# Second block's FFN norm and the hybrid's successor get a head that runs ahead of the norm; the wait for masks stands later

## The reference, cut to what matters

```python
def rms_norm(x, g):
    y = x * lax.rsqrt(jnp.mean(x * x, axis=-1, keepdims=True) + EPS)
    return y * g
# first block, each sublayer: x + (half of) (1 + gate) * f(h), with
#   h = rms_norm(x, g) * (1 + scale) + shift
# f in turn: swiglu, hybrid (LRU and SSD), swiglu; swiglu, mLSTM, swiglu
def swiglu(h, w_gate, w_up, w_down):
    return (jax.nn.silu(h @ w_gate) * (h @ w_up)) @ w_down
# second block, behind its branches:
#   x = x + gate1 * rms_norm(mix, norm_mix_post)
#   h = rms_norm(x, norm_ffn_pre) * (1 + scale2) + shift2
#   x = x + gate2 * rms_norm(relu(h @ w_ff1)**2 @ w_ff2, norm_ffn_post)
```

## Time and profile before

| | us |
|---|---|
| median of 3 runs | 3580.46 |
| lowest and highest | 3576.4, 3591.96 |
| the profiled execution | 3580.06 |
| its span | 3578.2 |
| TensorE busy in it | 3448.2 |
| VectorE busy | 2018.7 |
| ScalarE busy | 1212.7 |

### The profile page before, as it was taken

The page is one execution under the profiler, slowest core; times in us unless marked ns, Lnnn a source line. Parts: engine busy times, 40 slices in busy tenths (PEclk is TensorE's granted clock), DMA queues, the critical chain, the costliest instruction groups (busy, mean ns, idle before and its releaser), DMA issues. The chain is left out here.

```text
span 3578.2 us, 56582 instructions
## 1 busy us (share of the span) xinstructions
PE 3448.2 (96%) x22456; PEld 2780.9 (78%) x22456; DVE 2018.7 (56%) x2820; ACT 1212.7 (34%) x1783; POOL 360.7 (10%) x264
## 2 busy tenths in 40 slices
PE   7999999999999999999999999999988999999998
PEld 5888777878888788876678888877757787878886
DVE  6666666846665666575443433365666773464343
ACT  3222346432222322243343322233434543233231
POOL 1000003410000000000101000130103330010000
PEclk9999999999999999999999999999979999989999
DMA  6554321125553455421032222222210002223232
GB/s 246 197 193 169 125 76 71 55 93 188 188 207 139 179 191 203 156 86 54 1 112 88 96 97 106 84 88 83 63 33 6 8 6 73 95 65 100 89 99 71
DMA packets 103765, 382.75 MB, mean 107 GB/s; under 512 B 11424, under 2 KB 15136, under 8 KB 103200
## 3 DMA queue, kind: packets, MB, share of 16 engines
q1 hardware_dynamic: 103584, 380.15, 30.7%
HBM read 378.01 MB, written 2.10 MB: 106 GB/s over the span
## 5 line engine op out<-in xcount | busy, mean ns | idle before, releaser
L457 PE MATMUL bank<-h_hi,w_hi 128*128 128x512 f32 x2576 | 1015.5, 394 | 29.2 <-DVE w_lo L252 26.5
L459 PE MATMUL bank<-h_hi,w_lo 128*128 128x512 f32 x2576 | 1005.6, 390 | 0.0
L458 PE MATMUL bank<-h_lo,w_hi 128*128 128x512 f32 x2576 | 1005.3, 390 | 0.0
L252 DVE TENSOR_TENSOR w_lo<-w_raw,w_hi 128x1024 fp32r<-128x1024 f32 (+2 forms) x480 | 634.3, 1321 | 397.7 <-ACT w_hi L246 386.5
L246 ACT ACTIVATE w_hi<-w_raw 128x1024 fp32r<-128x1024 f32 (+2 forms) x475 | 521.1, 1097 | 299.8 <-PE bank L459 260.4
L457 PEld LDWEIGHTS bank<-h_hi,w_hi 128*128 128x128 f32 x2576 | 485.3, 188 | 146.5 <-DVE w_lo L252 30.0
L459 PEld LDWEIGHTS bank<-h_hi,w_lo 128*128 128x128 f32 x2576 | 485.0, 188 | 102.4
L458 PEld LDWEIGHTS bank<-h_lo,w_hi 128*128 128x128 f32 x2576 | 485.5, 188 | 100.7 <-issue 1.9
L457 PE MATMUL bank<-f_gu_hi,w_hi 128*128 128x512 f32 x704 | 278.5, 396 | 0.0
L458 PE MATMUL bank<-f_gu_lo,w_hi 128*128 128x512 f32 x704 | 278.2, 395 | 0.0
L459 PE MATMUL bank<-f_gu_hi,w_lo 128*128 128x512 f32 x704 | 278.2, 395 | 0.0
(11 more groups left out here) (645 smaller groups left out, 4759.4 us busy)
## 6 DMA issues: line engine op xcount, KB each, us to landing
ada_tiles<-in_ada SPq DMA_DIRECT2D x180, 512.0 KB, 4.3
w_raw<-in_gu SPq DMA_DIRECT2D x176, 512.0 KB, 4.4
w_raw<-in_dn SPq DMA_DIRECT2D x64, 704.0 KB, 5.0
w_raw<-in_w_ff SPq DMA_DIRECT2D x64, 512.0 KB, 3.5
w_raw<-in_w_hyb SPq DMA_DIRECT2D x36, 512.0 KB, 3.4
w_raw<-in_w_rkv SPq DMA_DIRECT2D x24, 512.0 KB, 3.5
w_raw<-in_w_attn SPq DMA_DIRECT2D x20, 512.0 KB, 3.5
w_raw<-in_w_hout SPq DMA_DIRECT2D x16, 512.0 KB, 3.4
```

The source lines that it names most:

```text
L252: K.nc.vector.tensor_tensor(K.w_lo[:, half, 0:kb * P], K.w_raw[:, slot, 0:kb * P], K.w_hi[:, half, 0:kb * P].bitcast(F32), ALU.subtract).t ...
L457: nc.tensor.matmul(K.ps[bank][:], wh, hi, start=start, stop=False)
L458: nc.tensor.matmul(K.ps[bank][:], wh, lo, start=False, stop=False)
L459: last_mm = nc.tensor.matmul(K.ps[bank][:], wl, hi, start=False, stop=stop)
```

## The change

Four things. The swiglu behind the hybrid gets an early head: the last gemm of the hybrid makes the halves of x times gain ahead, in two regions that the hybrid has left. The second block's FFN gets one too, of a new class: its gain stands in `K.coef`, its squares are added between the products of its early tile (four sums for each chunk), its row comes behind the tile, and `norm` makes the halves ahead, chunk by chunk. In `gemm`, every early head now has the split of tile 3 in turn t = 0, ahead of tile 0's evacuation. And the wait for the RWKV masks is only in front of TensorE's first use of them.

```diff
                     if head and isinstance(i, int) and t < 3:
-                        if t < 2 and not (early and t == 0):
+                        if early and t == 0:
+                            split_lo(K, dve, kb, 3 % RING, 1, g0 + 3)
+                        elif t < 2 and not early:
                             split_lo(K, dve, kb, (t + 2) % RING, t % SPLIT, g0 + t + 2)
...
-                    hi, lo, bank, start, stop = mm(c, 0)
+                    _, _, bank, start, stop = mm(c, 0)
+                    hi, lo = head.ahead_hi[:, c, :], head.ahead_lo[:, c, :]
...
+class SecondModulated(Modulated):
+    def between(self, pe, n):
+        K, c, part = self.K, n // 3, n % 3
+        if part == 0:
+            pe.wait_ge(K.sq_done.sem, K.sq_done(c + 1 - DC))
+        for t in ((0, 1), (2,), (3,))[part]:
+            last = K.nc.tensor.matmul(K.ps[self.SUM][:, t:t + 1], self.squares.sq[0][:, c % 2, t * P:(t + 1) * P], K.ones[:, 0:1],
+                                      start=c == 0 and t == 0, stop=c == DC - 1, skip_group_check=True)
+        if part == 2:
+            last.then_inc(K.sq_added.sem if c < DC - 1 else K.rms_sum.sem, 1)
+        if DC <= n < 2 * DC:
+            self.shift_part(pe, n - DC)
+
+    def behind(self, pe):
+        self.row_of_roots(pe)
...
-            if squares:
-                squares.add_by_pe(pe).then_inc(K.rms_sum.sem, 1)
...
-                    nc.scalar.activation(squares.sq[0][:, c % 2:c % 2 + 1, :], K.x[:, c:c + 1, :], ACT.Square).then_inc(K.sq_done.sem, 1)
+                    nc.scalar.activation(follow.squares.sq[0][:, c % 2:c % 2 + 1, :], K.x[:, c:c + 1, :], ACT.Square).then_inc(K.sq_done.sem, 1)
+                    follow.ahead_act(act, c)
...
                 v.tensor_tensor(K.x[:, c, :], K.x[:, c, :], t[:, c, :], ALU.add).then_inc(K.x_written.sem, 1)
+                if follow and c:
+                    follow.ahead_dve(dve, c - 1)
...
@@ hybrid, last gemm
             squares.by_act(act, K.x[:, o:o + 1, :], o, o % 2)
+            follow.ahead_act(act, o)
...
             v.scalar_tensor_tensor(x, K.ps[HOUT_BANK[o]][:], K.coef[:, o:o + 1], x, ALU.mult, ALU.add).then_inc(free.sem, 1)
+            follow.ahead_dve(dve, o)
...
@@ second block
-    norm(K, "n2p", mix, col(K, "mix_post", 0, 8), gate=gt1, squares=Squares(K, "x2", K.h_at + 4 * S * 4))
-    head = Modulated(K, col(K, "ffn_pre", 0, 8), sc2, sh2)
+    head = SecondModulated(K, col(K, "ffn_pre", 0, 8), sc2, sh2, Squares(K, "x2", A))
+    norm(K, "n2p", mix, col(K, "mix_post", 0, 8), gate=gt1, follow=head)
...
@@ rwkv
-            dve.wait_ge(loaded, 16)
-            pool.wait_ge(loaded, 16)
-            pe.wait_ge(loaded, 16)
...
             def key_squares(i, x):
+                if i == 0:
+                    pe.wait_ge(loaded, 16)
```

More of the change, by code:

```diff
@@ L620, in add @@
             K.nc.gpsimd.tensor_tensor(self.acc[n][:], self.acc[n][:], self.sq[n][:, slot, :], ALU.add).then_inc(K.sq_added.sem, 1)
[L622 to L632, removed]
     def advance_pe(self):
@@ L850, in advance, with __init__, gain_ahead @@
             c.base += DC
+class SecondModulated(Modulated):
+    GAIN_STEPS = 0
+    def __init__(self, K, gain, scale, shift, squares):
+        super().__init__(K, gain, scale, shift, early=True)
+        self.gain_at, self.squares = K.coef, squares
+    def gain_ahead(self, dve):
+        K = self.K
+        K.nc.vector.scalar_tensor_tensor(K.coef[:], self.scale, 1.0, self.gain, ALU.add, ALU.mult).then_inc(K.coef_done.sem, 1)
+        dve.wait_ge(K.coef_done.sem, K.coef_done(1))
+    def between(self, pe, n):
[11 more added lines that the diff above has]
+        self.row_of_roots(pe)
 class FirstModulated(Modulated):
@@ L1128, in pool, with norm @@
             K.nc.gpsimd.tensor_scalar(K.x[:, c, :], K.x[:, c, :], self.final[:, c:c + 1], None, ALU.mult)
-def norm(K, name, src, gain, gate, squares=None, store=None):
+def norm(K, name, src, gain, gate, follow=None, store=None):
     nc = K.nc
@@ L1146, in _ @@
             rms.rms_act(act)
-            if squares:
+            if follow:
+                act.wait_ge(K.coef_done.sem, K.coef_done(1))
                 for c in range(DC):
@@ L1164, in _ @@
             v.tensor_tensor(K.gain[:], gain, gate, ALU.mult).then_inc(K.x_written.sem, 1)
+            if follow:
+                follow.gain_ahead(dve)
             rms.rms_dve(dve)
@@ L1171, in _ @@
                 v.tensor_tensor(K.x[:, c, :], K.x[:, c, :], t[:, c, :], ALU.add).then_inc(K.x_written.sem, 1)
+                if follow and c:
+                    follow.ahead_dve(dve, c - 1)
+            if follow:
+                follow.ahead_dve(dve, DC - 1)
     rms.rms_advance()
@@ L1174, in norm @@
     K.scaled.base += DC
-    if squares:
-        squares.advance_pe()
+    if follow:
+        follow.squares.advance_pe()
+        follow.ahead_advance()
+        K.coef_done.base += 1
 def swiglu(K, name, w_gu, w_down, nxt, head, gate, ada=None, double=False, follow=None):
@@ L1384, with hybrid @@
         ("lo_l", "rows", DC), ("n_sum", "e", 1), ("n_root", "bc", 1), ("n_rs", "fin", 1), ("n_row", "hi", 1), ("scaled", "zeroed", DC), ("hi_s", "trig", DC)]
-def hybrid(K, nxt, head, gate):
+def hybrid(K, nxt, head, gate, follow):
     nc, d = K.nc, K.dram
@@ L1788, in hybrid @@
     squares = Squares(K, "hyb", A + 2 * DC * CH)
+    follow.ahead_hi = K.at("hyb_ahead_hi", [P, DC, S], F32R, A + GATE * CH)
+    follow.ahead_lo = K.at("hyb_ahead_lo", [P, DC, S], F32R, A + Z * CH)
     def out_mm(k, j):
@@ L3735, in build @@
                 follow = final_head(K)
-            elif step != "hyb":
+            else:
                 follow = Modulated(K, *terms(K, *places[plan[n + 1]]), early=True)
@@ L3740, in build @@
                 with stage(K):
-                    hybrid(K, nxt, head, gate)
+                    hybrid(K, nxt, head, gate, follow)
             elif step == "ml":
```

17 lines of the change are left out of this document (9 added, 8 removed).

## The result

| | before | after |
|---|---|---|
| median us (9 runs each) | 3582.31 | 3603.7 |
| lowest and highest | 3576.4, 3593.84 | 3599.68, 3616.41 |
| span of the profiled execution | 3578.2 | 3597.9 |
| granted clock over the span | 0.983 | 0.982 |

The ratio is 1.0057, 95% interval 1.0044 to 1.0070: 20.4 us slower (15.8 to 25.1). The prediction was 3607, range 3590 to 3617.

A forecast was written before the change was run, and what follows sets the result against it. TensorE was taken to bound the kernel, so only its waits and half clock counted. 8.5 + 0.8 + 0.2 + 8.8 + 11.7 - 2.7 = +27.3 us on 3580.06 gave 3607, range 3590 to 3617.

The forecast's parts named there:

- What bounds: Whole kernel: TensorE is the bound, busy for 3448.2 of 3578.2 us; all its waits together are 130 us.
- Part 1: Early heads of hybrid, second swiglu, mLSTM, attention: earlier-queued split leaves VectorE idle, tile 4 starts later, +8.5 us.
- Part 2: Swiglu behind the hybrid: early head with the new split order costs +0.8 us, plus 0.2 for a coefficient product.
- Part 3: Five early heads: two waits become one longer gap before tile 4, half clock follows, +8.8 us.
- Part 4: Norm before the second block's FFN: early tile between the sums runs at half clock, tile 4 later by 11.7 us.
- Part 5: Start of the RWKV loop: TensorE starts earlier, key sums then wait for the masks, -2.7 us.
- The sum: Whole kernel: all terms together +27.3 us on 3580.06, giving 3607.
- A: Second block's FFN norm: clock comes up inside the early tile, -0.8 us instead of +11.7, total 3594.9; chance 0.17.
- B: Early heads: tile 4 not late for VectorE's queue, no gaps or clock falls, +2.4 us, total 3582; chance 0.06.
- C: Early heads and second block's norm: A and B together, -10 us, total 3570, no slower; chance 0.04.
- D: Early heads and second block's norm: longest half clock and upper bound for the norm, +34.8 us, 3615; chance 0.08.

The follow-up runs named there:

- experiment 1: Parts alone against kernel before: order of splits 1.0043, masks 0.9991, second block's FFN norm 1.0028, hybrid's work ahead 0.9983; old order in changed kernel 0.9996.
- experiment 3: Changed kernel plus 12 unread 512-column products behind tile 3 of every early head: 3618.3 us, ratio 1.0080.

## Why the prediction was right, point by point

- **What bounds.** Right: every term is time in which TensorE waits or runs at half clock.
- **Part 1, tile 4 later.** Forecast 3.1 + 3 x 1.8 = 8.5; the table has 3.68 + 1.94 + 1.93 + 0.83 = 8.4. The idle time was foretold at 1.83 and is 1.86. The sum hides an error: attention (0.83, not 1.8) was taken after the hybrid without a row for its tile 4, and the second swiglu cost more. Its old 30.23 was a good draw: the old order took 29.9 to 33.0 in the other profiles, 31.0 on average over all ten with it.
- **Part 2.** +1.0 forecast, +1.17 found; without the new order the early head gives 1.9 back (128.1 on average against 130.0).
- **Part 3, the clock.** +8.8 forecast, 1.56 + 1.48 + 2.26 + 1.19 = 6.5 found. Over-sized, for attention's gap is 2.07 and not 3.4 and nothing fell there, and the swiglu behind the hybrid had one stretch of 3.4 us of half clock, not 4.7.
- **Part 4.** +11.7 forecast, +13.2 found. The early tile took 27.4 us, not 26.3: in a plain chunk three large products and four small ones take 2.98, so a small one costs 0.43, as in the earlier trace rows. The discount to 0.40, which I took from a row at full clock, isn't there at half clock. It also began 1.1 later. The wait for the low half (`L715`) in place of the second chunk is the least of it: the clock fell at 3188.7, ahead of the row of 1/rms at 3189.10, and in the kernel before at 3182.8, when its row was done. The row took 2.08 us (`L656` above), where the timeline of the kernel before has

```profile
3181.61 1.16 PE L663 MATMUL bank<-consts,rms_rs 128*128 128x128 f32 x8 [0.57 <-DVE rms_rs L689]
```

- **Part 5.** -2.7 forecast, -2.74 found.
- **The sum.** 8.4 + 1.2 + 6.5 + 13.2 - 2.7 = 26.6 against 27.3. The times say 20.4, 25.1 at most, and the two profiled executions 19.7. RWKV's turns make the difference: they are 7.1 us shorter in the changed one, and 26.6 - 7.1 = 19.5. The prediction put them at nothing ("The chain behind is serial, so this stays"). They go with the hybrid's head, as told under experiment 1; which thing in that edit shortens them was not tried, and one profile a kernel is what it rests on. Parts timed alone give -3.2 + 10.0 - 6.1 + 15.4 = 16.1, and 6.3 for the order in the two new heads, 22.4; each has an interval of 5 us up and down, and the -6.1 has the shorter turns in it.
- **The rivals.** A (the clock comes up in the early tile) did not happen: 0.50 over all 27 us. Its price was about right: with the clock held up by the unused products, the stretch gave 10.1 of the 12.5 us back. B and C fell with the gaps of 3.9 to 5.6 us, D with attention.
- **The step that fell short** is the reading of one profile as the kernel's state. I set the sum against a profiled execution without asking which of its stretches would repeat, or would move with an edit made far ahead of them. That 27.3 lies so near 26.6 is partly luck: the clock term was 2.3 too large and the norm's 1.5 too small.

## What to carry to other kernels

A split that needs a later tile must not be queued ahead of an evacuation that needs only an earlier one, on either of the engines that share the split: two waits of 1.7 and 1.0 us became 0.7 and 4.0, and a long gap costs again in the clock behind it. Laying work "between" others is worth the clock it runs at: before moving a large tile into a stretch of short products, read the granted clock there. Where a change moves a kernel by half a percent and its runs scatter by as much, compare stretches between fixed products over several profiles; and a row of one-column products on a busy TensorE is best laid among long ones.

## What the runs showed of the hardware that I had not expected

- TensorE busy for 27.00 of 27 us stayed at 1.2 GHz, and in the kernel with 38 unused products it fell to that between two chunks (3195) without a pause. With 42 long products added it stayed at 2.4 GHz, and finished 8.5 us sooner.
- Most of a kernel's scatter is the clock. In 35 runs of the kernel before, the time lost to it (the span times what the granted clock lacks to 1) goes from 57 to 76 us and the span from 3576 to 3596, and the two rise together (correlation 0.93, 0.98 us of span for each us lost). mLSTM's loop alone has two lengths, some 10 us apart, with 10.2 to 13.7 or 27.3 to 30.7 us of half clock in it, and the same code in it. With the short products spread it has 3.4 us, and the runs' range is 12.7 us where the same kernel without this had 16.9.
- RWKV's seven turns vary between 251.6 and 262.7 us. Half clock (13 to 24 us in them) explains part. TensorE also waits 0.5 to 1.9 us at a time where the profile shows no releaser, and mostly in the same places in kernels of one kind: 7 or 8 such waits, 7.5 to 9.0 us together, in the five kernels without the hybrid's new head, 3 to 5, 2.5 to 4.2 us together, in eight with it, and 9 of 9.2 us in that of experiment 3. In the traces' DMA records all 80 of them end 2.2 to 2.9 us behind the start of a packet of 16 KB on the queue that the profile calls "instruction"; 52 or 53 such packets start in the seven turns, one in 5 us. It looks as if TensorE waits there for its own code, and as if an edit far ahead moves the places where it has to; neither was tried.
